# A triangular inverse by levels: 32-column moving operands in place of 64-column ones

## The reference

```python
def step(S, inp):
    r_t, w_t, k_t, v_t, kk_t, a_t = inp
    sa = jnp.einsum('bhvk,bhk->bhv', S, kk_t)
    S = (S * w_t[:, :, None, :]
         - sa[..., None] * (kk_t * a_t)[:, :, None, :]
         + v_t[..., None] * k_t[:, :, None, :])
    y = jnp.einsum('bhvk,bhk->bhv', S, r_t)
    return S, y
```

## Time and profile before

| what | value |
|---|---|
| median of 3 runs | 2551.86 us (2550.63 to 2555.51) |
| profiled execution, its own time | 2550.62 us |
| its span (first to last instruction) | 2548.8 us |
| TensorE busy | 2470.7 us (97%) |
| VectorE, ScalarE, GpSimd busy | 1544.3, 1202.8, 78.2 us |
| level, pair and chunk matmuls with both operands in the regions (L682) | 3072 records, 103.7 us |
| TensorE idle before them | 8.5 us |

### The profile page before, as it was taken

One profiled execution on the slowest core, in us unless ns is written; L12 is line 12 of the kernel. 1 busy time (PEld: TensorE's weight loads), 2 busy tenths in 40 slices (PEclk: granted clock), 3 DMA queues, 4 the chain that ended last, 5 costly groups with the idle time before them and its releaser, 6 DMA issues.

```text
span 2548.8 us, 54008 instructions
## 1 busy us (share of the span) xinstructions
PE 2470.7 (97%) x22769; PEld 2356.4 (92%) x22769; DVE 1544.3 (61%) x1835; ACT 1202.8 (47%) x1516; POOL 78.2 (3%) x69
## 2 busy tenths in 40 slices
PE   7999999999999999999999999999999999999997
PEld 7999999899999889999899999999999888999886
DVE  7577576645774445555769886564855444554444
ACT  4676343222454446664573344446545333444342
POOL 0000023400000000000000000000000000000000
PEclk9999999999999999999999999999999999999999
DMA  8355542221546565455456655455566556666554
GB/s 262 125 173 174 173 135 85 89 81 53 183 144 191 186 189 152 149 178 177 141 167 189 182 164 171 161 167 181 157 190 191 189 186 186 184 187 184 188 187 134
DMA packets 215959, 419.73 MB, mean 165 GB/s; under 512 B 16832, under 2 KB 19216, under 8 KB 215040
## 3 DMA queue, kind: packets, MB, share of 16 engines
q1 hardware_dynamic: 207232, 397.46, 50.7%
q0 software_dynamic: 2016, 10.07, 1.2%
q10 hardware_dynamic: 6512, 9.28, 1.1%
HBM read 410.47 MB, written 6.29 MB: 164 GB/s over the span
## 4 chain that ended last, share of the span: by engine, by line
PE 88%; DVE 6%; ACT 3%; issue 1%; DMA 1%; POOL 0%; SPq 0%; DVEq 0%; ACTq 0%
PE ps L473 26%; PE ps L474 26%; PE ps L475 26%; PE ps L682 6%; DVE wlo L343 2%; ACT whi L339 1%; PE ps L732 1%; PE ps L586 1%; PE ps L600 1%; DMA regions<-in_xT 0%; DMA regions<-in_a_a 0%; DVE act_lo L1857 0%; PE ps L832 0%; POOL regions L435 0%; ACT regions L1314 0%
## 5 line engine op out<-in xcount | busy, mean ns | idle before, releaser
L343 DVE TENSOR_TENSOR wlo<-wraw,whi 128x1024 fp32r<-128x1024 f32 x752 | 930.1, 1241 | 863.6 <-ACT whi L339 862.6
L473 PE MATMUL ps<-act_hi,whi 128*128 128x256 f32 (+1 forms) x4736 | 1358.2, 287 | 36.7 <-DVE act_lo L1968 12.7
L474 PE MATMUL ps<-act_lo,whi 128*128 128x256 f32 (+1 forms) x4736 | 1339.5, 283 | 0.0
L475 PE MATMUL ps<-act_hi,wlo 128*128 128x256 f32 (+1 forms) x4736 | 1337.9, 283 | 0.0
L339 ACT ACTIVATE whi<-wraw 128x1024 fp32r<-128x1024 f32 x752 | 793.9, 1059 | 1127.0 <-PE ps L475 1119.4
L473 PEld LDWEIGHTS ps<-act_hi,whi 128*128 128x128 f32 x4736 | 898.2, 190 | 44.0 <-issue 27.0
L474 PEld LDWEIGHTS ps<-act_lo,whi 128*128 128x128 f32 x4736 | 901.1, 190 | 1.2
L475 PEld LDWEIGHTS ps<-act_hi,wlo 128*128 128x128 f32 x4736 | 898.2, 190 | 0.0
L475 PE MATMUL ps<-whi,regions_r 128*128 128x512 f32 x512 | 203.0, 396 | 0.0
L474 PE MATMUL ps<-wlo,regions_r 128*128 128x512 f32 x512 | 203.0, 396 | 0.0
L473 PE MATMUL ps<-whi,regions_r 128*128 128x512 f32 x512 | 203.0, 396 | 0.0
(11 more groups left out here) (307 smaller groups left out, 1577.8 us busy)
## 6 DMA issues: line engine op xcount, KB each, us to landing
wraw<-in_a_w_in SPq DMA_DIRECT2D x128, 512.0 KB, 3.8
wraw<-in_w_up SPq DMA_DIRECT2D x128, 512.0 KB, 3.9
wraw<-in_w_down SPq DMA_DIRECT2D x128, 512.0 KB, 4.4
wraw<-in_w_in SPq DMA_DIRECT2D x112, 512.0 KB, 3.8
wraw<-in_b_w_qg SPq DMA_DIRECT2D x64, 512.0 KB, 3.8
wraw<-in_a_w_out SPq DMA_DIRECT2D x32, 512.0 KB, 4.3
wraw<-in_w_k_shared SPq DMA_DIRECT2D x32, 512.0 KB, 4.4
wraw<-in_w_v_shared SPq DMA_DIRECT2D x32, 512.0 KB, 4.7
```

What stands on the lines that cost most here:

```text
L343: nc.vector.tensor_tensor(wlo[:, q % RING], wraw[:, q % RING], whi[:, q % RING].bitcast(F32), ALU.subtract).then_inc(lo_ready, 1)
L473: mm(o, hi_s, hi_m, start=first, stop=False, skip_group_check=True)
L474: mm(o, hi_s, lo_m, start=False, stop=False, skip_group_check=True)
L475: i = mm(o, lo_s, hi_m, start=False, stop=last, skip_group_check=True)
```

## The change

The diagonal 32x32 blocks of the inverse are all that levels 0 to 4 fill, so the two blocks of a head are laid side by side in rows and share 32 columns: `Tp` and `Tm` become 256 columns for each f where they were 512, and so does `Yl`. The y and z steps are now `narrow`: 64x64 stationary operands as before, 32 moving columns. At level 5 the stationary operand of z is `Yl` with 32 columns, and the product has 32 rows. `ab` is as it was, and so is everything on GpSimd but one semaphore.

`TTs`, the stationary operand of z, must still be 64x64. For levels 2 to 5 ScalarE lays it out from `Tp` in two copies with a per-partition scale of 1 or 0 (`halves`), ahead of its copy of y. VectorE's pair step is four operations in place of two. Its z operations have 256 columns.

```diff
+    parts["ident32"] = (p[:, None] % HB == np.arange(HB)[None, :]) * 1.0
+    parts["halves"] = np.stack([p % CH < HB, p % CH >= HB, -1.0 * (p % CH < HB)], 1) * 1.0
...
-        AB, Bm, Tm, Yl = (R[:, 1, 1024 * i:1024 * (i + 1)] for i in range(4))
+        AB, Bm = (R[:, 1, 1024 * i:1024 * (i + 1)] for i in range(2))
+        Tp, Tm, Yl = (R[:, 1, 2048 + 512 * i:2560 + 512 * i] for i in range(3))
...
                         if lv == 1:
-                            pool.wait_ge(S["lv_t"], n_ - 1)
+                            pool.wait_ge(S["tt_pair"], 2 * c + f + 1)
...
+            def narrow(f, o_bank, lhs, rhs, m_rows):
+                for j in range(8 * f, 8 * f + 8):
+                    for hs in (0, N):
+                        m_ = mm(ps[hs:hs + m_rows, o_bank, (j % 8) * HB:(j % 8 + 1) * HB], lhs[hs:hs + N, j * m_rows:(j + 1) * m_rows],
+                                rhs[hs:hs + N, j * HB:(j + 1) * HB], start=True, stop=True)
+                return m_
...
-                    pairs(f, 4 + f, (flat(Bm), flat(Tm))).then_inc(S["lv_y"], 1)
+                    narrow(f, 4 + f, Bm, Tm, N).then_inc(S["lv_y"], 1)
                 if kind == "z":
                     pe.wait_ge(S["lv_ysb"], m_ + 1)
-                    pe.wait_ge(S["lv_t"], n_ - 1)
-                    pairs(f, 6 + f, (tt_, flat(Yl)) if lv < 5 else (flat(Yl), tt_)).then_inc(S["lv_z"], 1)
+                    if lv == 1:
+                        pe.wait_ge(S["tt_pair"], 2 * c + f + 1)
+                    else:
+                        pe.wait_ge(S["lv_t"], LV_T(c, f, lv - 1))
+                    (narrow(f, 6 + f, TTs[:, c], Yl, N) if lv < 5 else narrow(f, 6 + f, Yl, Tp, HB)).then_inc(S["lv_z"], 1)
...
                 if kind == "y":
                     n_, m_ = (c * 6 + lv) * 2 + f, (c * 5 + lv - 1) * 2 + f
+                    if lv > 1:
+                        act.wait_ge(S["tp_ready"], (c * 4 + lv - 2) * 2 + f + 1)
+                        whole = both_halves(TTs[:, c], f)
+                        for b in range(2):
+                            st.do(a(whole[:, :, b, :], packed_half(Tp, f), ACT.Copy, scale=cs("halves")[:, b:b + 1]), sig["lv_t"] if b else None)
...
-                    st.do(a(Yl[:, f * GW:(f + 1) * GW], bank(4 + f), ACT.Copy), sig["lv_ysb"])
+                    if m_ >= 2:
+                        act.wait_ge(S["lv_z"], m_ - 1)
+                    st.do(a(Yl[:, f * 256:(f + 1) * 256], ps[:, 4 + f, 0:256], ACT.Copy), sig["lv_ysb"])
...
                     dve.wait_ge(S["lv_b"], n_ + 1)
-                    st.do(tt(heads(TTs[:, c, fs], 8), i8, heads(Bm[:, fs], 8), ALU.subtract), sig["lv_t"])
+                    pair = both_halves(Bm, f)
+                    st.do(tt(packed_half(Tp, f), pair[:, :, 0, :], pair[:, :, 1, :], ALU.add))
+                    st.do(tt(heads(TTs[:, c, fs], 8), i8, heads(Bm[:, fs], 8), ALU.subtract), sig["tt_pair"])
+                    st.prev(2)
+                    st.do(tt(packed_half(Tp, f), i32, packed_half(Tp, f), ALU.subtract))
                     st.prev()
-                    st.do(nc.vector.transpose(Tm[:, fs], TTs[:, c, fs]), sig["lv_m"])
+                    st.do(nc.vector.transpose(Tm[:, 256 * f:256 * (f + 1)], Tp[:, 256 * f:256 * (f + 1)]), sig["lv_m"])
```

More of the change, by code:

```diff
@@ L27 @@
 CH = 64
+HB = 32
 LORA = 96
@@ L160, in program @@
             act_step dve_step gi_ready ss_done sq_ready rn_ready rnr_ready rnx_ready rnx_bc bcm_ready rk_ready rk_bc vt_mm
-            v_ready bvs_ready bv_stored0 bv_stored1 bv_loaded0 bv_loaded1 silu_ready gate_stored gate_loaded0 gate_loaded1 ab_mm ab_ready am_mm am_ready tok_mm tok_ready lv_b lv_y lv_ysb lv_z
+            v_ready bvs_ready bv_stored0 bv_stored1 bv_loaded0 bv_loaded1 silu_ready gate_stored gate_loaded0 gate_loaded1 ab_mm ab_ready am_mm am_ready tok_mm tok_ready tp_ready tt_pair tt_done lv_b lv_y lv_ysb lv_z
             lv_m lv_t gn_var gn_std w_mm w_sb u_mm u_sb y_mm y_sb m_mm m_sb yn_ready zt_mm z1_ready z_ready z_f
@@ L251, in program @@
         TTs = R[:, 0, :].rearrange("p (c n) -> p c n", c=4)
-        AB, Bm, Tm, Yl = (R[:, 1, 1024 * i:1024 * (i + 1)] for i in range(4))
+        AB, Bm = (R[:, 1, 1024 * i:1024 * (i + 1)] for i in range(2))
+        Tp, Tm, Yl = (R[:, 1, 2048 + 512 * i:2560 + 512 * i] for i in range(3))
+        packed_half = lambda t_, f: t_[:, 256 * f:256 * (f + 1)].rearrange("p (h t) -> p h t", h=8)
+        both_halves = lambda t_, f: t_[:, GW * f:GW * (f + 1)].rearrange("p (h b t) -> p h b t", h=8, b=2)
         AM = wk(0, 3072).rearrange("p (j a t) -> p j a t", j=KT, a=3)
@@ L269, in program @@
                     level_steps += [("z", c, f, lv)] + [("ab", c + 1, f, 0)] * (lv == 5 and c < 3)
+        LV_T = lambda c, f, lv: (c * 4 + lv - 1) * 2 + f + 1
         steps_at, at_ = [], 0
@@ L691, in level @@
                 ts = slice(c * CH, (c + 1) * CH)
-                tt_ = flat(TTs[:, c])
                 if kind == "ab":
@@ L721, in _ @@
             pe.wait_ge(S["silu_ready"], 4)
-            pe.wait_ge(S["lv_t"], 48)
+            pe.wait_ge(S["tt_done"], 8)
             for it in range(4):
@@ L1157, in level @@
                     act.wait_ge(S["lv_y"], m_ + 1)
-                    act.wait_ge(S["lv_t"], n_ - 1)
-                    st.do(a(Yl[:, f * GW:(f + 1) * GW], bank(4 + f), ACT.Copy), sig["lv_ysb"])
+                    if m_ >= 2:
+                        act.wait_ge(S["lv_z"], m_ - 1)
+                    st.do(a(Yl[:, f * 256:(f + 1) * 256], ps[:, 4 + f, 0:256], ACT.Copy), sig["lv_ysb"])
             for s in range(4):
@@ L1692, in _ @@
             i8 = cs("ident64").unsqueeze(1).broadcast_to([P, 8, CH])
+            i32 = cs("ident32").unsqueeze(1).broadcast_to([P, 8, HB])
             def level(kind, c, f, lv):
@@ L1705, in level @@
                         dve.wait_ge(S["bv_stored0"], 32)
+                    if c:
+                        dve.wait_ge(S["lv_t"], LV_T(c, f, 0))
                     dve.wait_ge(S["lv_b"], n_ + 1)
-                    st.do(tt(heads(TTs[:, c, fs], 8), i8, heads(Bm[:, fs], 8), ALU.subtract), sig["lv_t"])
+                    pair = both_halves(Bm, f)
[3 more added lines that the diff above has]
+                    st.do(tt(packed_half(Tp, f), i32, packed_half(Tp, f), ALU.subtract))
                     st.prev()
-                    st.do(nc.vector.transpose(Tm[:, fs], TTs[:, c, fs]), sig["lv_m"])
+                    st.do(nc.vector.transpose(Tm[:, 256 * f:256 * (f + 1)], Tp[:, 256 * f:256 * (f + 1)]), sig["lv_m"])
                 if kind == "z" and lv < 5:
                     dve.wait_ge(S["lv_z"], m_ + 1)
-                    st.do(tt(Tm[:, fs], Tm[:, fs], bank(6 + f), ALU.subtract), sig["lv_m"])
+                    st.do(tt(packed_half(Tm, f), packed_half(Tm, f), ps[:, 6 + f, 0:256].rearrange("p (h t) -> p h t", h=8), ALU.subtract), sig["lv_m"])
                     st.prev()
-                    st.do(nc.vector.transpose(TTs[:, c, fs], Tm[:, fs]), sig["lv_t"])
+                    if lv > 1:
+                        dve.wait_ge(S["lv_t"], LV_T(c, f, lv - 1))
+                    st.do(nc.vector.transpose(Tp[:, 256 * f:256 * (f + 1)], Tm[:, 256 * f:256 * (f + 1)]), sig["tp_ready"])
                 if kind == "z" and lv == 5:
                     dve.wait_ge(S["lv_z"], m_ + 1)
-                    st.do(tt(TTs[:, c, fs], TTs[:, c, fs], bank(6 + f), ALU.subtract), sig["lv_t"])
+                    right = both_halves(TTs[:, c], f)[:, :, 1, :]
+                    st.do(stt(right, ps[:, 6 + f, 0:256].rearrange("p (h t) -> p h t", h=8), cs("halves")[:, 2:3], right, ALU.mult, ALU.add),
+                          sig["tt_done"])
             for s in range(4):
```

## The result

The changed kernel takes 2572.18 us (median of 4 runs, 2570.37 to 2575.73) where the kernel before takes 2552.59 us: the ratio is 1.0076, with a 95% interval of 1.0063 to 1.0088. It is slower by 19.6 us, and outside the range that was forecast, 2547 to 2561 us. The profiled execution has a span of 2568.6 us, 19.8 us more than before.

The account below looks back on a forecast made before the run. TensorE, busy 97% of the span, was taken as the bound. Terms -2.5 - 1.1 + 0.5 + 5.4 + 1.5 = +3.8 us on the median of 2551.86 gave 2555.7 us, range 2547 to 2561.

Parts of the forecast that it names:

- The steps: 72 y and z steps of levels 1 to 4: 64 stationary columns still need 56 ns for two records, -2.5 us.
- z of level 5: Steps with 32 stationary and 32 moving columns: up to 27 ns less of each 58, five of eight counting, -1.1 us.
- the changes of shape: On TensorE between z of level 5 and ab, six changes of matmul shape, at most 0.15 us each: +0.5 us.
- The chain: VectorE and GpSimd at each chunk's beginning: the longer pair step makes y f1 of level 1 start 1.33 us later, +5.4 us.
- Never run together: At chunk beginnings, a GpSimd mask and a VectorE operation with both inputs in SBUF take turns, the later waiting for the earlier.
- The clock: At chunk ends: longer waits lower TensorE's clock at one of two spared ends, 1.5 us; +1.5 us, bounds 0 to +3.0.
- What costs nothing: ScalarE's layouts ahead of z have 0.6 us of cover, and VectorE's z operations halve: no time added.
- The slower side: Chunk beginnings: GpSimd goes ahead of the second subtraction (+7.3) and the clock falls at both spared ends (+3.0); 2559 us, chance 0.27.
- The first two rivals: Narrow steps: moving columns set the pace (2541 us, chance 0.10), or something between needs about 50 ns (2549 us, 0.05).
- the loads' distance: Sign that the forecast is right: weight loads in the 32-column steps 55 to 58 ns apart for two.
- the idle time: Sign that the forecast is right: TensorE's idle time before the steps rises from 8.5 us to 13 to 16.
- theory A: From the experiments: a wait lowers the clock, and 32-column steps are too little work to win it back, so it stays low.

Follow-up runs that it names:

- e1_wide: The changed kernel with each narrow y and z matmul streaming its 32 columns twice, so 64 moving columns: 2557.28 us, ratio 1.0012.
- e4b_filler: The changed kernel with unread filler matmuls on TensorE while it waits for the first y of a chunk: 2548.92 us, ratio 0.9982.
- e11_cols32_long: The kernel before with 32 moving columns in y and z and the longer pair step, no packed layout or ScalarE copies: 2582.56 us, ratio 1.0091.
- e8_narrow_early: The changed kernel with VectorE masking level 0 from PSUM and doing each half's pair step right behind its ab: 2550.57 us, ratio 0.9997.
- e5_wide_y: The changed kernel with 64 moving columns again in the y steps alone, 32 in the z steps: 2553.88 us, ratio 1.0005.
- e2_cols32: The kernel before with y and z matmuls streaming only the first 32 of their 64 columns, pair step as before: 2559.11 us, ratio 1.0029.
- e3_long_pair: The kernel before with two more 256-column VectorE operations in each pair step, results overwritten: 2557.44 us, ratio 1.0019.
- e7_early_pair: The kernel before with VectorE masking level 0 from PSUM and doing each half's pair step right behind its ab: 2549.56 us, ratio 0.9984.

## Why the prediction was wrong, point by point

- **The steps, -2.5 us.** The reading was right that the 64 stationary columns hold the pace when the moving ones are halved, and that the two sides stand nearly level (54 ns with only the moving side at 64). Its size was 0 by the loads, 58.5 ns for two after and 58.2 before, and at most -0.9 us by the distance of the step pairs (3.60 in place of 3.62 us, 36 times). The 112 ns of L617 halved to 56 was 2.5 ns too little.
- **z of level 5, -1.1 us, and the changes of shape, +0.5.** The loads took the whole of their bound, 31 ns for two in place of 58: -2.2 us for five. The changes of shape took about what was put. Together they are read from the start of such a step to the next product of the weights: 1.70 us (401.85 to 403.55) in place of 2.01, so 5 x 0.31 = -1.5 us where -0.6 was put. The Trainium skill's TensorE: Matmul & The Clock Gate (section Wait — 56ns, not 53.3ns?) has a floor of about 25 ns between starts. These loads average 31 ns for two, so that floor does not hold across two quarters of the array.
- **The chain, +5.4 us.** Right in kind, half in size. (Four times the computed 1.33 is 5.3.) From the start of the last z step to y f1 it is 410.67 - 401.85 = 8.82 us after and 407.92 - 399.85 = 8.07 before: +0.75 for each of three chunks where 1.33 was computed. The first chunk's wait grew by 0.72 (3.67 and 0.25 against 3.20). VectorE's and GpSimd's timelines at this place show the turns, of which one direction was read rightly:

```profile
405.24 0.42 DVE L1733 TENSOR_TENSOR regions<-regions 128x256 f32<-128x256 f32 x1
405.57 1.59 DVE L1734 TENSOR_TENSOR regions<-cst,regions 128x512 f32<-128x512 f32 x1
407.08 0.41 DVE L1736 TENSOR_TENSOR regions<-cst,regions 128x256 f32<-128x256 f32 x1
...
407.90 0.83 DVE L1733 TENSOR_TENSOR regions<-regions 128x256 f32<-128x256 f32 x1
```

```profile
405.40 1.20 POOL L442 TENSOR_TENSOR regions<-regions,cst 128x512 f32<-128x512 f32 x1 [3.17 <-DVE regions L1724]
407.24 1.21 POOL L442 TENSOR_TENSOR regions<-regions,cst 128x512 f32<-128x512 f32 x1 [0.63 <-DVE regions L1734]
```

  The subtraction L1734 lasted 1.59 us behind the mask of 405.40. But GpSimd did not wait for the operation with 256 columns: the mask of 407.24 started beside L1736 and lasted 1.21 us, only 0.12 more than alone, where it had been put behind that operation, 0.4 later. "Never run together" was too strong. The idle time rose by 4.2 us in all.
- **The clock, +1.5 us with a bound of +3.0.** This is the step that failed. The place and the trigger were named, and one more place was expected to be caught; the price of a fall was taken from the one short stretch before, 1.5 us, as if it did not depend on the steps that follow. At the chunk of 408 us the steps from y f1 to 434.53 take 23.86 us where the same steps at the full clock take 2.68 + 3 x 3.61 = 13.5: +10.4. The chunk of 507 us lost 10.3, and the one of 462 us 1.5. The fall before at the earlier trace rows had cost 1.5. That makes 10.4 + 10.3 + 1.5 - 1.5 = +20.7 us, where +1.5 was put. The mean clocks say the same without any timeline. What is missing from full speed, times the span, is the time lost: 0.021 x 2568.6 - 0.013 x 2548.8, some 21 us (an estimate, since waits count in it too). The rest is small and cancels in part. The first chunk adds 2.2 us, clock and wait together (its z of level 1 starts 17.24 us after the ab step in place of 15.06), and the three chains 2.2; z of level 5 takes off 1.5. At the last z step of the inverses the changed kernel is 23.7 us behind (551.56 against 527.84), at the end 19.8: about 1.7 of that came back because the kernel before had one more low stretch behind the inverses, 0.77 and 0.80 from 544 to 552 us, and some 1.6 was not traced. e1_wide, e4b_filler and e11_cols32_long show the cause from three sides: give back the columns, take away the waits, or put both into the other kernel.
- **What costs nothing.** Right. ScalarE's layouts last 0.495 us each, and in no row does TensorE wait for them; the experiment without them lost as much or more.
- **The rivals.** The slower side had the right pair of causes, the longer turns and the clock at two spared chunk ends, and was itself a short stretch per fall: 2559 us where 2572 came. The first two rivals, in which narrow steps run faster, are out by the 58.5 ns. Of the signs named, the loads' distance (58.5 ns against 55 to 58) and the idle time (12.7 us against 13 to 16) came out just beside their ranges; GpSimd as the releaser, the later y and the low clock at more chunk ends came as said.

What stays open is why the same waits and the same steps are followed by a long stretch at one place and a short one at another. In the profiled executions the clock stayed low for over 10 us behind 2 of 3 chunk ends in the changed kernel, 3 of 3 in e8_narrow_early and in e11_cols32_long, 1 of 3 in e5_wide_y, but 0 of 3 in e2_cols32 with its narrow steps and short waits. With 64 columns in y and z (before, e1_wide, e3_long_pair, e7_early_pair) it was 0 of 12. Behind the first chunk's wait it was 7 us or less in every execution, narrow steps or not, which theory A does not explain. That it depends on where the waits fall in time was not tried.

## What to carry to other kernels

Before halving the moving columns of small matmuls, look at what spaces their starts: if the stationary side holds the same pace, halving one side gives next to no time and makes TensorE do less per microsecond; here only both sides halved gave anything. A price taken from a short fall of the clock holds only for the instructions that followed it there; if a change thins those out, the stretch may last many times longer. A wait of one to two microseconds ahead of thin work is worth filling with matmuls whose result nothing reads, or shortening: both together took this change from 0.76% slower to 0.37% faster.

## What the runs showed of the hardware

- The same instruction count at the same pace, with 32 in place of 64 moving columns, changed how long the granted clock stayed at its lower level after a wait: some 24 us in the changed kernel and e11_cols32_long at most chunk ends, against 7 or less in e1_wide (0.63 and 0.52 over two windows of 4 us) and e3_long_pair. Not each time: one chunk end of the changed kernel and the three of e2_cols32 had 3 to 4 us.
- At the lower clock two weight loads of 64 columns needed 105 ns in place of 58.5: the loads follow the clock as well.
- With 64x64 float32 steps in two quarters of the array, two records started every 58 ns with 64 stationary and 64 or 32 moving columns, every 54 with 32 stationary and 64 moving (e1_wide), and every 31 with 32 of both.
- Waits far shorter than the stretches of low clock that followed came before them: 1.86 and 1.05 us ahead of 24 us in the changed kernel, a single one of 1.37 us in e8_narrow_early. The same waits did not bring them in every execution.
- A GpSimd operation and a VectorE one with two inputs in SBUF took turns fully when the GpSimd one was first (0.68 us became 1.59), and nearly not when VectorE's 256-column one had started 0.16 us before (1.09 became 1.20 and 1.21).
